# A hybrid attention block on one core: neighbourhood attention on array halves, wide probabilities scaled before they are transposed, and four more conditioning slices on TensorE

## The chip, the cores and the metric

The kernel runs on one core of one Trainium2 chip. The metric is the device time of a whole execution in microseconds (us), lower being better. The engines are TensorE (PE in the profile; PEld is its weight load), VectorE (DVE), ScalarE (ACT), GpSimd (POOL) and SyncE (SP, which only issues transfers here).

## The reference, cut to what matters

A stream of 256 latent tokens follows 256 context tokens through 4 layers of width 1024. Layers 0 and 3 mix tokens by neighbourhood attention, layer 1 by retention, layer 2 by a convolution, and each is followed by a convolutional feed-forward part. A conditioning vector gives shift, scale and gate of every part.

```python
def na_mixer(hx, hc, w_qkv, w_o, q_gain, k_gain, rpb, need_ctx):   # 16 heads of 64
    q, k, v = heads(h @ w_qkv); q, k = head_rms_norm(q), head_rms_norm(k)
    # a latent token sees its neighbourhood (with a bias from rpb) and all context tokens
    s_nb  = einsum('bhqd,bhqkd->bhqk', q_r, k_nb) * NA_SCALE + bias_r
    s_ctx = einsum('bhqd,bhkd->bhqk', q_r, kc) * NA_SCALE
    p = softmax(concatenate([s_nb, s_ctx], axis=-1))
    o = einsum(p[..., :nb], v_nb) + einsum(p[..., nb:], vc)
    yx = merge_heads(o) @ w_o
    # a context token sees all context tokens (needed in layer 0 only)
    p = softmax(einsum('bhqd,bhkd->bhqk', qc, kc) * NA_SCALE)
    yc = merge_heads(einsum(p, vc)) @ w_o
```

## The kernel before, in words

Activations lie with features on the 128 partitions and 512 tokens along the free axis: columns 0 to 255 are the context (`CT`), 256 to 511 the latent tokens (`XT`). Tokens form four blocks `b` of 128, of which 0 and 1 are context ("narrow": 256 keys) and 2 and 3 latent ("wide": 512 keys). Every projection is three fp32r products (high x high, low x high, high x low); SP brings weights in groups of 512 KB into four slots `raw`, ACT writes the high part `Whi` (line 1009) and DVE the low part `Wlo` (line 1339). Each engine's program is written out by hand, and its order is the order in which things run; semaphores tie the engines together.

**Projections of attention.** The q/k stage makes 16 tiles of 128 features (`head_sum`, line 731, sums squares of a head; DVE's `normed`, lines 1530 and 1532, normalises). It runs as four rounds of four tiles `m` with a normalisation behind each. V follows token-major (lines 581 to 583).

**Attention.** A head pair `i` (8 of them) is one row group of `QK`: head `par` = 0 in partitions 0 to 63, `par` = 1 in 64 to 127. A unit is (`par`, `b`); in layer 0 a head pair has 8 units, in layer 3 (latent tokens only) 4. For a unit POOL copies half the queries into `Qz`, whose other half is zero (line 517); PE multiplies over all 128 rows (line 762); DVE adds the bias `rel` (wide units, line 1560) and takes the negated maximum (line 1562); ACT writes the exponentials with their sum (line 1138); PE transposes them in blocks of 128 (line 770); ACT copies the result to `probT` (line 1130); PE multiplies `probT` as weights by 64 columns of `V` (line 780); DVE takes the reciprocal of the sum (line 1568) and scales into `O` (line 1570). Units run one by one, the transposes two units and the last product three units behind the scores. After the last head pair `O` is transposed (line 814), split into `Hhi` (ACT, line 1165) and `Hlo` (DVE, line 1595), and the o projection (lines 575 to 577) begins.

**Conditioning.** Its weights come in 512 KB pieces. The first slices of 128 features are made on PE at the start: line 674 uses a quarter of the columns for each piece of a product of 32x512, and line 680 transposes the result. All other pieces are "weighs" on DVE (line 1363, over 1024 columns), with a scaling on POOL (line 461) and a sum on ACT (line 1026). The constants `IN_V`, `IN_HEADS` and `IN_O` place 8 weighs in layer 0's V stage, 8 in its attention (one to a head pair) and 8 in its o projection; four weighs are one slice. The norm behind the o projection (lines 453, 455, 688 to 699) opens the feed-forward part.

## Time and profile before

| what | value |
|---|---|
| runs (three) | 2615.69 to 2620.32 us, median 2619.65 |
| time of the profiled execution / its span | 2620.63 / 2618.7 us |
| PE, PEld busy | 96%, 80% of the span |
| DVE, ACT, POOL busy | 72%, 40%, 21% |
| matrix instructions | 12948 |

The profiled execution's own time is 0.98 us above the median of the runs. Rows below give a start in us from the span's start, a duration in us, and the engine; "x4" means four instructions joined in one row, of which the duration covers all. Such durations overlap the next row on PE, since matrix products are pipelined: what a group costs is the distance from its start to the next group's start.

### The profile page before, as it was taken

Reading aid. Unit: us, or ns where it says so; the run is one execution under the profiler, and the core shown is the slowest. Engines: PE = TensorE matmul, PEld = TensorE weight load, DVE = VectorE, ACT = ScalarE, POOL = GpSimd, SP = SyncE. Lnnn points to the kernel's source line nnn. Section 1 sums busy time; section 2 is a strip of 40 time slices with the busy share of each in tenths; the row PEclk is TensorE's granted clock in tenths of the full one; section 3 lists DMA queues with packets and bytes.
Section 4 is the critical chain, followed back from the end, with each engine's and each line's share of the span. In section 5 each row is a group of like instructions: output and inputs, shape, how many; then the busy total and the mean of one; then the engine's idle time right before and its main releaser. Section 6 shows DMA issues by size and latency. Waiting matters only on the chain. (4 is left out here: it accounts for less than half of the span.)

```text
span 2618.7 us, 37653 instructions
## 1 busy us (share of the span) xinstructions
PE 2521.8 (96%) x12948; PEld 2093.5 (80%) x12948; DVE 1887.9 (72%) x2765; ACT 1044.2 (40%) x1677; POOL 557.3 (21%) x367
## 2 busy tenths in 40 slices
PE   6999989999999999999999999999999999999999
PEld 4777778888888857788888887878888887777999
DVE  4887789888974344427888768877988777756874
ACT  2336714444231123314444226543444323344543
POOL 5123243332210020022333210003333224002000
PEclk8999989999999999999999999989999999999999
DMA  8332034545632311223445531103544545311455
GB/s 265 99 123 79 32 129 143 174 167 197 210 117 96 107 62 49 88 97 137 174 168 170 188 119 57 57 17 113 169 168 169 193 155 125 105 41 65 169 184 178
DMA packets 94883, 337.39 MB, mean 129 GB/s; under 512 B 11840, under 2 KB 13632, under 8 KB 94656
## 3 DMA queue, kind: packets, MB, share of 16 engines
q1 hardware_dynamic: 64832, 231.99, 25.9%
q10 hardware_dynamic: 27072, 95.13, 10.9%
q0 software_dynamic: 2880, 8.92, 1.7%
q8 instruction: 66, 1.08, 0.2%
q14 instruction: 33, 0.27, 0.0%
HBM read 334.95 MB, written 1.05 MB: 128 GB/s over the span
## 5 line engine op out<-in xcount | busy, mean ns | idle before, releaser
L575 PE MATMUL bank<-Hhi,Whi 128*128 128x512 f32 (+1 forms) x2440 | 879.8, 361 | 46.9 <-DVE Wlo L1339 20.2
L576 PE MATMUL bank<-Hlo,Whi 128*128 128x512 f32 (+1 forms) x2440 | 863.2, 354 | 0.0
L577 PE MATMUL bank<-Hhi,Wlo 128*128 128x512 f32 (+1 forms) x2440 | 863.0, 354 | 0.0
L1339 DVE TENSOR_TENSOR Wlo<-raw,Whi 128x1024 fp32r<-128x1024 f32 x424 | 638.6, 1508 | 243.1 <-ACT Whi L1009 241.1
L1009 ACT ACTIVATE Whi<-raw 128x1024 fp32r<-128x1024 f32 x424 | 448.2, 1059 | 793.6 <-DMA raw<-in_weights 710.9
L575 PEld LDWEIGHTS bank<-Hhi,Whi 128*128 128x128 f32 x2440 | 467.4, 192 | 123.3 <-issue 41.1
L576 PEld LDWEIGHTS bank<-Hlo,Whi 128*128 128x128 f32 x2440 | 467.7, 192 | 65.9 <-issue 4.8
L577 PEld LDWEIGHTS bank<-Hhi,Wlo 128*128 128x128 f32 x2440 | 467.2, 191 | 62.2
L461 POOL TENSOR_TENSOR cond_w<-cond_w,cond 128x1024 f32<-128x1024 f32 x115 | 276.8, 2407 | 559.3 <-DVE square L1363 516.6
L575 PE MATMUL bank<-Ghi,Whi 128*128 128x512 f32 (+1 forms) x770 | 269.5, 350 | 0.0
L577 PE MATMUL bank<-Ghi,Wlo 128*128 128x512 f32 (+1 forms) x770 | 268.8, 349 | 0.0
L576 PE MATMUL bank<-Glo,Whi 128*128 128x512 f32 (+1 forms) x770 | 268.3, 348 | 0.0
L453 POOL TENSOR_TENSOR square<-X 128x512 f32<-128x512 f32 (+1 forms) x58 | 84.8, 1463 | 689.0 <-DVE X L1481 680.1
L1363 DVE SCALAR_TENSOR_TENSOR hb<-cond_w,cond 128x1024 f32<-128x1024 f32 x138 | 185.8, 1346 | 4.7
L576 PEld LDWEIGHTS bank<-Glo,Whi 128*128 128x128 f32 x770 | 144.5, 188 | 21.5
L575 PEld LDWEIGHTS bank<-Ghi,Whi 128*128 128x128 f32 x770 | 144.5, 188 | 21.4
L577 PEld LDWEIGHTS bank<-Ghi,Wlo 128*128 128x128 f32 x770 | 144.4, 188 | 21.2
L1287 ACT ACTIVATE hb<-hb 128x512 f32<-128x512 f32 (+1 forms) x88 | 51.0, 579 | 218.7 <-DVE hb L1794 218.7
L1026 ACT ACTIVATE cond_w<-cond_w 128x1024 f32<-128x1024 f32 x115 | 121.0, 1052 | 36.2 <-POOL cond_w L461 35.6
L1363 DVE SCALAR_TENSOR_TENSOR square<-cond_w,cond 128x1024 f32<-128x1024 f32 x99 | 121.2, 1224 | 11.7
L581 PE MATMUL bank<-Whi,Hhi 128*128 128x512 f32 x256 | 101.3, 396 | 2.6 <-DVE QK L1532 2.6
L1481 DVE SCALAR_TENSOR_TENSOR X<-bank,mod,X 128x256 f32<-128x256 f32 x84 | 37.4, 478 | 90.5 <-PE bank L577 90.4
(202 smaller groups left out, 3118.8 us busy)
## 6 DMA issues: line engine op xcount, KB each, us to landing
raw<-in_weights SPq DMA_DIRECT2D x424, 512.0 KB, 3.3
cond_w<-in_ada ACTq DMA_DIRECT2D x176, 512.0 KB, 3.8
ada_raw<-in_ada SPq DMA_DIRECT2D x16, 512.0 KB, 15.6
rel_in<-in_rpb POOLq DMA_DIRECT2D x48, 128.0 KB, 4.7
decay_t<-in_dist POOLq DMA_DIRECT2D x4, 640.0 KB, 4.2
X<-in_x ACTq DMA_DIRECT2D x1, 2048.0 KB, 9.6
out_y<-X SPq DMA_DIRECT2D x1, 1024.0 KB, 4.8
cos_sin<-in_rope ACTq DMA_DIRECT2D x1, 256.0 KB, 2.5
```

The lines of the kernel that those rows point to most:

```text
L453: g.tensor_tensor(square[:, c % 2, tok], X[:, c, tok], X[:, c, tok], ALU.mult).then_inc(sum_step, 1)
L461: g.tensor_tensor(w, w, cond[:, 0, :], ALU.mult).then_inc(cond_scaled, 1)
L575: t.matmul(dst, Whi[:, st.slot, w], hi, start=start, stop=False)
L576: t.matmul(dst, Whi[:, st.slot, w], lo, start=False, stop=False)
L577: return t.matmul(dst, Wlo[:, st.slot, w], hi, start=False, stop=stop)
L581: t.matmul(dst, hi, Whi[:, st.slot, w], start=start, stop=False)
L1009: a.activation(Whi[:, st.slot, :], raw[:, st.slot, :], ACT.Copy).then_inc(hi_split, 1)
L1026: a.activation(w, w, ACT.Copy, accum_out=cond_sum[:, n % COND_SLOTS, 0:1]).then_inc(cond_summed, 1)
L1287: a.activation(cv[:, k, tok], cv[:, k, tok], ACT.Gelu_apprx_tanh).then_inc(gelu_done, 1)
L1339: v.tensor_tensor(Wlo[:, st.slot, :], raw[:, st.slot, :], Whi[:, st.slot, :].bitcast(F32), ALU.subtract)\
L1363: last = v.scalar_tensor_tensor(spare[:, :, :].rearrange("p k t -> p (k t)"), w, 1.0, cond[:, r, :], ALU.mult, ALU.mult, accum_out=cond_su ...
L1481: last = v.scalar_tensor_tensor(X[:, m, hs], src[:, hs], gate, X[:, m, hs], ALU.mult, ALU.add)
```

## The change

Attention is planned by a class `Heads`: units in the order head pair, block, head, so that the two heads of one block stand next to each other. A step works on such a pair of units.

- Scores are taken straight from `QK`, head 0 from partitions 0 to 63 and head 1 from 64 to 127, each over half of the array's rows; `Qz` and its copies go.
- For wide units one DVE operation adds the bias, negates, and takes the minimum (`tensor_tensor_reduce`, over 512 keys, the bias of the context keys being zeros); ACT's exponential has scale -1 there. Narrow units keep their reduction.
- The reciprocal is taken of the two sums of a step at once, and the probabilities are scaled before the transposes: wide ones by DVE in place, narrow ones by POOL.
- ACT copies the transposed wide units, DVE the narrow ones. The last product has 64 columns of `V` as weights and 256 queries as moving columns, head 0 into the upper half of a bank's partitions and head 1 into the lower: its result already has features on partitions. `O` and its transposes go; `out_high` and `out_low` split each result while attention runs.
- Transposes stand three steps behind the scores, and the last product of a head pair's stream follows every second step.
- Four more slices of conditioning (`ADA_QK`) go to PE, one in each of the four rounds of layer 0's q/k stage: `ada_slice` (8 products of 32 columns by 512, four of them side by side on column quarters) behind tile 1, its transposes ahead of the last `head_sum`; SP loads 2 MB for each. DVE copies the rows and stores them (`ada_rows`, `ada_store`). PE waits for the last store ahead of V. The 8 weighs in attention and the 8 in the o projection go (`IN_HEADS`, `IN_O`), and ACT loads the first conditioning pieces only behind `ada_used` of the fourth slice.
- In layer 0 ACT evicts V's blocks 2 and 3 (`evict_v`), which DVE did. The convolution's filter is loaded at the start of retention.

```diff
-ADA_FIRST = 4
+ADA_START = 4
+ADA_QK = 4
+ADA_FIRST = ADA_START + ADA_QK
 QUAD = P // 4
 COND_SLOTS = 3
 PER_LAP = 3
 IN_V = 8
-IN_HEADS = 8
-IN_O = (0, 0, 1, 1, 2, 2, 3, 4)
+IN_HEADS = 0
+IN_O = ()
...
+    def __init__(self, layer):
+        self.last = layer == DEPTH - 1
+        self.blocks = (2, 3) if self.last else (0, 1, 2, 3)
+        self.units = [(i, par, b) for i in range(C) for b in self.blocks for par in range(2)]
+        self.n = len(self.units)
+        self.u0 = 8 * C if self.last else 0
+        self.wide0 = 4 * C if self.last else 0
+        per = 2 * len(self.blocks)
+        self.ends = {n: (n // per, 0 if n % 8 == 3 and not self.last else 1) for n in range(3, self.n, 4)}
...
-                        pool.wait_ge(scored, SCORED0 + u0 - n_units + n_units // 2 * (par + 1) + n_units * i)
-                        half = slice(64 * par, 64 * par + 64)
-                        g.tensor_copy(Qz[half, par, tok], QK[half, i, tok]).then_inc(q_staged, 1)
...
+                h = Heads(layer)
+                for n, (i, par, b) in enumerate(h.units):
+                    if b < 2:
+                        pool.wait_ge(inverted, h.u0 // 2 + n // 2 + 1)
+                        g.tensor_scalar(prob[n % 6][:, CT], prob[n % 6][:, CT], rinv[:, n // 2 % 4, par:par + 1], None,
+                                        ALU.mult).then_inc(narrow_scaled, 1)
...
+            def ada_slice(n):
+
+                for k in range(C):
+                    if k % 2 == 0:
+                        pe.wait_ge(ada_loaded[k // 2], 16 * (n + 1))
+                    last = ada_product(bank[6], k, ada_ring[:, k // 2, 512 * (k % 2):512 * (k % 2) + 512])
+                last.then_inc(ada_used, 1)
...
+                            if layer == 0 and n < ADA_QK and m == 1:
+                                ada_slice(n)
+                            if layer == 0 and n < ADA_QK and m == 3:
+                                ada_cols(ADA_START + n)
                         head_sum(3, 8 * nth + 3 + 4 * i, tok)
+                if layer == 0:
+                    pe.wait_ge(mod_ready, 4 * ADA_FIRST)
                 tokens_major(p["v"], 2, p["mix_tile"] + 16)
 
 
...
-                    pe.wait_ge(exped, u0 + u + 1 + n_units * i)
-                    t.matmul(bank[u % 4][:, keys], Qz[:, par, P * b:P * b + P], QK[:, 8 + i, keys],
+                    half = slice(64 * par, 64 * par + 64)
...
+                    if n >= 4:
+                        pe.wait_ge(exped, h.u0 + n - 3)
+                    t.matmul(bank[n % 4][:, keys], QK[half, i, P * b:P * b + P], QK[half, 8 + i, keys],
                              start=True, stop=True).then_inc(scored, 1)
...
+                def turn(n):
+                    i, par, b = h.units[n]
+                    if b < 2:
+                        pe.wait_ge(narrow_scaled, h.narrow(n))
+                    else:
+                        pe.wait_ge(wide_scaled, h.wide(n))
+                    if n >= 2:
+                        copies(n - 2)
+                    for kb in range(2 if b < 2 else TB):
...
+                    turned = wide_pT[:, h.parity(i), :, :, :] if stream else narrow_pT
+                    n_keys = TB if stream else 2
                     for kb in range(n_keys):
-                        last = t.matmul(bank[6 + u % 2][:, 0:NA_HD], probT[:, u % 2, P * kb:P * kb + P],
-                                        V[:, kb, bass.ts(2 * i + par, NA_HD)], start=kb == 0, stop=kb == n_keys - 1)
+                        for par in range(2):
+                            last = t.matmul(bank[h.out_bank(i, stream)][64 * par:64 * par + 64, 0:CTX],
+                                            V[:, kb, NA_HD * (2 * i + par):NA_HD * (2 * i + par + 1)],
+                                            turned[:, par, kb, :], start=kb == 0, stop=kb == n_keys - 1)
...
+                for s in range(h.n // 2 + 4):
+                    if s == 0:
+                        pe.wait_ge(tile_free, FREE0 + p["mix_tile"] + 2 * C + TB)
+                    if s == 1:
+                        pe.wait_ge(tile_free, FREE0 + p["mix_tile"] + 2 * C + 2 * TB)
+                    for n in (2 * s, 2 * s + 1):
+                        if n < h.n:
+                            scores(n)
+                    for n in (2 * s - 6, 2 * s - 5):
+                        if 0 <= n < h.n:
+                            turn(n)
+                    if 2 * s - 7 in h.ends:
+                        attend(2 * s - 7)
...
+                def evict_v(y):
+                    act.wait_ge(weights_used, p["v"] + 4 * y + 4)
+                    for b in (2, 3):
+                        a.activation(V[:, b, 512 * y:512 * (y + 1)], bank[V_BANKS[y][b]][:, :], ACT.Copy)\
+                            .then_inc(v_made, 1)
...
+                    act.wait_ge(ada_used, ADA_QK)
+                    for n in range(COND_SLOTS):
+                        load_weights(n)
...
+                def exponentials(n):
+                    i, par, b = h.units[n]
...
+                    act.wait_ge(peaked, h.u0 + n + 1)
+                    if n >= 6:
+                        act.wait_ge(p_turned, h.u0 + n - 5)
+                    a.activation(prob[n % 6][:, keys], bank[n % 4][:, keys], ACT.Exp, bias=peak[:, n % 4:n % 4 + 1],
+                                 scale=1.0 if b < 2 else -1.0, accum_out=psum_p[:, n // 2 % 4, par:par + 1]).then_inc(exped, 1)
+
+                def out_high(n):
+                    i, stream = h.ends[n]
+                    act.wait_ge(attended, h.u0 // 4 + n // 4 + 1)
+                    a.activation(Hhi[:, i, XT if stream else CT], bank[h.out_bank(i, stream)][:, 0:CTX], ACT.Copy)\
+                        .then_inc(h_hi, 1)
+
+                for s in range(h.n // 2 + 5):
+                    for n in (2 * s, 2 * s + 1):
+                        if n < h.n:
+                            exponentials(n)
+                    if 2 * s - 9 in h.ends:
+                        out_high(2 * s - 9)
+                    for n in (2 * s - 6, 2 * s - 5):
+                        if 0 <= n < h.n and h.units[n][2] >= 2:
+                            copy_turned(n)
...
+                            if layer == 0 and n < ADA_QK and m == 2:
+                                ada_rows(n)
                             if m:
                                 normed(m - 1, k - 1, i, tok)
+                        if layer == 0 and n < ADA_QK:
+                            ada_store(ADA_START + n)
...
-                        sx = bank[u % 4][:, XT].rearrange("p (r k) -> p r k", k=GRID_W)
-                        v.tensor_tensor(sx, sx, rel[:, 2 * i + par, a0:a0 + 4, :], ALU.add).then_inc(biased, 1)
-                        dve.wait_ge(biased, b0 + 2 * par + b - 1 + x_units * i)
-                    v.tensor_reduce(peak[:, u % 4:u % 4 + 1], bank[u % 4][:, keys], axis=AX, op=ALU.max,
-                                    negate=True).then_inc(peaked, 1)
...
-                    v.tensor_scalar(O[:, i, b, NA_HD * par:NA_HD * (par + 1)], bank[6 + u % 2][:, 0:NA_HD],
-                                    rinv[:, u % 4:u % 4 + 1], None, ALU.mult).then_inc(o_stored, 1)
...
+                        sx = bank[n % 4][:, :].rearrange("p (s k) -> p s k", s=2)
+                        v.tensor_tensor_reduce(sx, sx, bias, -1.0, 3e38, ALU.add, ALU.min,
+                                               accum_out=peak[:, n % 4:n % 4 + 1]).then_inc(peaked, 1)
+                    else:
+                        v.tensor_reduce(peak[:, n % 4:n % 4 + 1], bank[n % 4][:, keys], axis=AX, op=ALU.max,
+                                        negate=True).then_inc(peaked, 1)
...
+                def invert_sums(s):
+                    dve.wait_ge(exped, h.u0 + 2 * s + 2)
+                    if s >= 4 and h.units[2 * s - 8][2] < 2:
+                        dve.wait_ge(narrow_scaled, h.narrow(2 * s - 7))
+                    v.reciprocal(rinv[:, s % 4, :], psum_p[:, s % 4, :]).then_inc(inverted, 1)
+                    if h.units[2 * s][2] >= 2:
+                        dve.wait_ge(inverted, h.u0 // 2 + s + 1)
+                        for par in range(2):
+                            p = prob[(2 * s + par) % 6]
+                            v.tensor_scalar(p, p, rinv[:, s % 4, par:par + 1], None, ALU.mult).then_inc(wide_scaled, 1)
...
+                    v.tensor_copy(narrow_pT[:, par, :, P * b:P * b + P],
+                                  bank[4 + n % 2][:, CT].rearrange("p (k q) -> p k q", q=P)).then_inc(narrow_copied, 1)
...
+                for s in range(h.n // 2 + 5):
+                    if 2 * s < h.n:
+                        peaks(2 * s)
+                    if 2 * s < h.n:
+                        peaks(2 * s + 1)
+                    if 0 < s <= h.n // 2:
+                        invert_sums(s - 1)
+                    for n in (2 * s - 6, 2 * s - 5):
+                        if 0 <= n < h.n and h.units[n][2] < 2:
+                            copy_turned(n)
+                    if 2 * s - 9 in h.ends:
+                        out_low(2 * s - 9)
```

On PE, at the end of the q/k stage, where V begins (before; `na_sq` holds squares, `Whi` the V weights from here on as moving operand):

```order
L575 MATMUL bank<-Hhi,Whi 128x512
L576 MATMUL bank<-Hlo,Whi 128x512
L577 MATMUL bank<-Hhi,Wlo 128x512
L731 MATMUL bank<-na_sq,one_head 128x512 x2
L151 REGISTER_ALU
L151 COMPARE_AND_BRANCH
L581 MATMUL bank<-Whi,Hhi 128x512
L582 MATMUL bank<-Whi,Hlo 128x512
```

The same place after the change:

```order
L616 MATMUL bank<-Hhi,Whi 128x512
L617 MATMUL bank<-Hlo,Whi 128x512
L618 MATMUL bank<-Hhi,Wlo 128x512
L780 MATMUL bank<-na_sq,one_head 128x512
L729 MATMUL bank<-ident,hb 128x128 x4
L780 MATMUL bank<-na_sq,one_head 128x512
L622 MATMUL bank<-Whi,Hhi 128x512
L623 MATMUL bank<-Whi,Hlo 128x512
```

The two products with `na_sq` now have four transposes of conditioning rows (`hb`) between them, and the first product of V stands behind a wait for DVE's last store.

On PE within layer 0's attention, before (one unit's scores, an earlier unit's transposes, a still earlier unit's last product, in turns):

```order
L770 MATMUL bank<-ident,prob 128x128 x4
L780 MATMUL bank<-V,probT 128x64 x2
L762 MATMUL bank<-QK,Qz 128x256
L770 MATMUL bank<-ident,prob 128x128 x4
L780 MATMUL bank<-V,probT 128x64 x4
L762 MATMUL bank<-QK,Qz 128x512
L770 MATMUL bank<-ident,prob 128x128 x2
L780 MATMUL bank<-V,probT 128x64 x4
L762 MATMUL bank<-QK,Qz 128x512
```

After the change (`square`, `root`, `total` and `hb` are here names under which the six probability buffers appear):

```order
L814 MATMUL bank<-QK 128x512 x2
L833 MATMUL bank<-ident,square 128x128 x8
L814 MATMUL bank<-QK 128x512 x2
L833 MATMUL bank<-ident,root 128x128 x2
L833 MATMUL bank<-ident,total 128x128 x2
L847 MATMUL bank<-wide_pT,V 64x256 x8
L814 MATMUL bank<-QK 128x256 x2
L833 MATMUL bank<-ident,hb 128x128 x4
L814 MATMUL bank<-QK 128x256 x2
L833 MATMUL bank<-ident,square 128x128 x8
```

Two scores now follow each other, then the transposes of two units, and only every second step has products of the last kind, with 256 columns in place of 64.

On DVE within layer 0's attention, before:

```order
L1570 TENSOR_SCALAR O<-bank,rinv 128x64
L1560 TENSOR_TENSOR bank<-bank,rel 128x256
L1562 TENSOR_REDUCE peak<-bank 128x1
L1568 RECIPROCAL rinv<-psum_p 128x1
L1570 TENSOR_SCALAR O<-bank,rinv 128x64
L1560 TENSOR_TENSOR bank<-bank,rel 128x256
L1562 TENSOR_REDUCE peak<-bank 128x1
L1568 RECIPROCAL rinv<-psum_p 128x1
```

After the change ("ISA" is the fused operation, and the row behind it reads its result back):

```order
L1634 RECIPROCAL rinv<-psum_p 128x2
L1653 TENSOR_TENSOR Hlo<-bank,Hhi 128x256
L1624 ISA bank,peak<-bank,rel 128x512
L1624 ISA peak 128x1
L1624 ISA bank,peak<-bank,rel 128x512
L1624 ISA peak 128x1
L1634 RECIPROCAL rinv<-psum_p 128x2
L1639 TENSOR_SCALAR hb<-hb,rinv 128x512 x2
L1646 COPY narrow_pT<-bank 128x2x128 x2
```

The addition and the reduction of a wide unit are one operation; the scaling moved from 64 columns of the result to 512 of the probabilities; copies of narrow units and the low part of the result are new here.

## Rows read from the trace of the kernel before

**Rows 1.** The page's busy times: engine, us, share of the span, instructions.
```profile
PE 2521.8 (96%) x12948; PEld 2093.5 (80%) x12948; DVE 1887.9 (72%) x2765; ACT 1044.2 (40%) x1677; POOL 557.3 (21%) x367
```

**Rows 2.** Windows: us, PE, PEld, DVE, ACT, POOL, PEclk, DMA share, GB/s.
```profile
142.00:174.00 32.00, 32.00 (x135) 24.92 (x134) 27.29 (x19) 9.07 (x12) 3.72 (x3) 1.00 0.25 87
207.00:212.00 5.00, 3.98 (x9) 2.48 (x9) 2.48 (x7) 3.56 (x7) 2.31 (x4) 0.50 0.35 129
208.00:316.00 108.00, 107.36 (x698) 85.92 (x699) 81.93 (x245) 79.53 (x212) 28.37 (x24) 0.98 0.13 44
```

**Rows 3.** Timeline of PE in layer 0's attention.
```profile
240.37 0.65 PE L762 MATMUL bank<-QK,Qz 128*128 x2
240.86 0.60 PE L770 MATMUL bank<-ident,prob 128*128 128x128 f32 x4
241.30 0.56 PE L780 MATMUL bank<-V,probT 128*128 x4
241.69 0.65 PE L762 MATMUL bank<-QK,Qz 128*128 x2
...
242.62 1.00 PE L780 MATMUL bank<-V,probT 128*128 x8
243.46 1.08 PE L762 MATMUL bank<-QK,Qz 128*128 x2
244.37 0.38 PE L770 MATMUL bank<-ident,prob 128*128 128x128 f32 x2
...
253.53 0.65 PE L762 MATMUL bank<-QK,Qz 128*128 x2
```

**Rows 4.** Groups of DVE in attention: shapes, count | busy us, mean ns | idle before.
```profile
L1562 DVE TENSOR_REDUCE peak<-bank 128x1 f32<-128x512 f32 x32 | 22.1, 691 | 1.1
...
L1560 DVE TENSOR_TENSOR bank<-bank,rel 128x256 f32<-128x256 f32 x32 | 13.8, 432 | 11.9 <-PE bank L762 11.0
L1562 DVE TENSOR_REDUCE peak<-bank 128x1 f32<-128x256 f32 x32 | 13.4, 418 | 2.1 <-PE bank L762 2.0
...
L1363 DVE SCALAR_TENSOR_TENSOR hb<-cond_w,cond 128x1024 f32<-128x1024 f32 x8 | 9.8, 1225 | 0.3
```

**Rows 5.** Timeline of PE at the first conditioning slices.
```profile
26.13 2.00 PE L674 MATMUL bank<-ada_raw,csilu 128*32 128x512 f32 x16
28.06 0.66 PE L680 MATMUL bank<-ident,rows 128*128 128x128 f32 x4
```

**Rows 6.** Groups of DVE in the convolution layer.
```profile
L1706 DVE TENSOR_SCALAR Wc<-U,cvf 128x512 f32<-128x512 f32 x8 | 3.9, 485 | 1.1 <-DVEq L1700 0.3
```

**Rows 7.** Timeline of DVE, then of POOL, behind the o projection.
```profile
361.00 2.18 DVE L1363 SCALAR_TENSOR_TENSOR hb<-cond_w,cond 128x1024 f32<-128x1024 f32 x1
...
359.76 2.34 POOL L455 TENSOR_TENSOR total<-total,square 128x512 f32<-128x512 f32 x1
```

**Rows 8.** Timeline of PE, then of DVE, where V begins.
```profile
157.98 1.55 PE L731 MATMUL bank<-na_sq,one_head 128*128 128x512 f32 x3
...
163.96 0.75 DVE L1532 SCALAR_TENSOR_TENSOR QK<-bank,qk_gain,na_root 128x512 f32 x1 [0.15 <-DVE na_root L1530]
```

**Rows 9.** Timelines: first exponential and first o product, layer 0, then layer 3.
```profile
210.13 0.47 ACT L1138 ACTIVATE prob<-bank,peak 128x256 f32<-128x256 f32 x1
...
323.68 0.50 PE L575 MATMUL bank<-Hhi,Whi 128*128 128x512 f32 x1 [1.73 <-DVE Hlo L1595]
...
2319.16 0.69 ACT L1138 ACTIVATE prob<-bank,peak 128x512 f32<-128x512 f32 x1 [3.45 <-DVE peak L1562]
...
2391.95 0.39 PE L575 MATMUL bank<-Hhi,Whi 128*128 128x256 f32 x1 [0.93 <-DVE Hlo L1595]
```

**Rows 10.** Timelines of PE: end of the o projection's norm, layer 0; the same stage, layer 2.
```profile
393.21 0.70 PE L699 MATMUL bank<-root,one 128*128 128x256 f32 x2 [0.24 <-DVE root L1398]
...
1756.80 0.77 PE L575 MATMUL bank<-Hhi,Whi 128*128 128x512 f32 x1 [3.10 <-DVE Hlo L1739]
...
1813.96 0.70 PE L699 MATMUL bank<-root,one 128*128 128x256 f32 x2 [0.24 <-DVE root L1398]
```

287 lines of the change are left out of this document (117 added, 170 removed).

## The prediction

> **What bounds the kernel now.** I read the page first. PE is busy for 96% of the span, DVE for 72%, ACT for 40% and POOL for 21% [rows 1]: a change pays where it takes work from PE, or where it ends a wait of PE. The windows say whether that holds stage by stage. In the q/k stage PE is busy for 32.00 of 32.00 us with DVE at 27.29, so anything put on PE there is paid in full; in layer 0's attention PE is busy for 107.36 of 108.00 us, with DVE at 81.93 and ACT at 79.53 [rows 2]. So attention before is a PE stage too.
>
> The timeline then prices each kind of work in it, by the distance from one group's start to the next's [rows 3]: wide scores 0.91 us (243.46 to 244.37), narrow scores 0.49 (240.37 to 240.86), four transposes 0.44 (240.86 to 241.30), hence two of them 0.22, the last product of a narrow unit 0.39 (241.30 to 241.69), of a wide one 0.84 (242.62 to 243.46). A head pair is 4 x (0.91 + 0.44 + 0.84) + 4 x (0.49 + 0.22 + 0.39) = 13.16 us, and the trace has 253.53 - 240.37 = 13.16. From the first exponential to the first o product it is 323.68 - 210.13 = 113.55 us in layer 0 and 2391.95 - 2319.16 = 72.79 in layer 3 [rows 9].
>
> **The change part by part.**
>
> *Four slices on PE in the q/k stage.* A slice has 8 products of 32 columns, four of them side by side. Before, 16 matmul records (8 products of two passes each) take 28.06 - 26.13 = 1.93 us up to the transposes [rows 5]; that is two rounds of four at the 0.91 of a product over 512 columns [rows 3], and about 0.1 left for going over to another kind. I add 0.44 for the transposes and 0.45 for four changes of kind into and out of the tiles. 4 x 2.8 = +11.2 us; without the changes it would be +9.5, with 0.25 each +13.5. No wait hides it, since PE has none there [rows 2]. SP's 8 MB more come on DMA queues at a share of 0.25. DVE's copies and stores, some 1.5 us a slice, fit beside its 27.29 of 32.
>
> *The wait ahead of V.* PE now stands until the fourth slice is stored, and this store is behind the third normalisation on DVE. PE's last squares end at about 159.5 (157.98 + 1.55), the normalisation at 164.7 (163.96 + 0.75) [rows 8]; with the wait for its input and a store of 0.6, PE starts at 165.3: 5.8 us idle. Behind a similar hole the granted clock is 0.50 in 207 to 212, the 1.2 GHz level of the two [rows 2], so I add 2 us: +7.8. The bounds are +5.8 and +10. Behind PE's wait stands all of V, and nothing else can go ahead of it.
> The Trainium skill ("TensorE: Matmul & The Clock Gate", Part 1) says too that an idle TensorE falls to its lower clock and has to be busy before it is given back; the trace agrees by that 0.50.
>
> *Attention of layer 0.* Per head pair PE does: scores of two heads on row halves. If they run side by side, two wide for the time of one: 2 x 0.91 + 2 x 0.49 = 2.80. Transposes stay: 4 x 0.44 + 4 x 0.22 = 2.64. The last products move 256 columns in two halves of the array's columns: four pairs for the latent stream and two for the context, each at the 0.49 of a product over 256 columns [rows 3]: 2.94. Ten changes between row halves, whole array and column halves at 0.15 add 1.5. Sum 9.9 us, 2.5 a step. No row shows row halves; column quarters side by side are in [rows 5], which is why I take the overlap, with both bounds kept.
> The Trainium skill ("TensorEngine Tiling (Array Packing)", "Key Properties") says that a change of tiling mode drains the engine. By the trace it costs 0.1 us at most at the one place where it happens [rows 5]; at nothing the step would be 2.1 us on PE, and VectorE would set it.
>
> DVE per head pair: four fused operations. Bounds are one pass of the reduction, 0.69, and the two operations it replaces, 0.43 + 0.69 = 1.12 [rows 4]. I take the lower, since it is one pass over 512 columns, and 0.08 for reading its result: 3.08. Four narrow reductions at 0.42 [rows 4] 1.68, four reciprocals at 0.15 0.6, four wide scalings at 0.485 from SBUF [rows 6] 1.94, four narrow copies and two low parts, each 256 columns and put at that 0.42, 2.52. Sum 9.8 us, 2.45 a step. ACT keeps its exponentials and loses half of its copies, so it stays below its 79.53 of 108. POOL has two narrow scalings in every second step, and they are wanted two steps later.
> PE and DVE are then equal, and each waits for the other through four banks of scores. I put the step at 2.7 us. With 32 steps, and 7.5 us for the last step's exponentials, scaling, transposes, copies, product and splitting: 31 x 2.7 + 7.5 = 91.2 against 113.55, -22.3 us. The transposes of `O`, and the 1.73 us ahead of the first o product [rows 9], go with it, since the split is made under way.
>
> *The o projection of layer 0* loses 8 weighs. The same stage with no weighs, in layer 2, takes 1813.96 - 1756.80 = 57.2 us from its first product to its norm's last; in layer 0 it takes 393.21 - 323.68 = 69.5 [rows 10, 9]. -12.3 us. It can't be more, as the rest is PE's own products; it could be some 3 less if other waits there stay.
>
> *Attention of layer 3.* Only wide units, 16 steps of two. PE per head pair: 1.82 + 1.76 + 1.96 + 5 x 0.15 = 6.3; DVE 4 x (0.77 + 0.485) + 0.3 + 0.42 = 5.7. Step 3.15 and 2.87; I take 3.3. 15 x 3.3 + 7.5 = 57 against 72.79: -15.8 us.
>
> *What costs nothing.* V's blocks are evicted by ACT, which is a quarter busy there; the convolution's filter arrives more than 1000 us before its use; the first conditioning pieces are fetched at about 158, and DVE has its first use near 170. Were that cover gone, the first weigh would be late by the transfer, a few us on DVE, not on PE.
>
> Sum: 11.2 + 7.8 - 22.3 - 12.3 - 15.8 = -31.4. From the profiled execution's 2620.6 that is 2589, or 2588 against the median of the runs, which is 1 us lower.
>
> **The rivals.**
>
> *Even faster (0.14).* DVE's minimum sets the step in layer 0 (2.45) and PE's in layer 3 (3.1), with changes of mode nearly free: -30.1 and -18.8, sum -42, 2578.
>
> *VectorE becomes the bound (0.09).* For it: it is 2.45 of a 2.5 us step. Either the fused operation takes its upper bound, 1.12 plus 0.08, which gives steps of 2.9 and 3.75; or its operations from SBUF stand while POOL works, as a weigh took 2.18 us beside POOL's addition [rows 7] against a mean of 1.23 [rows 4]. Together I put steps at 3.1 and 4.1: -10 and -3.8, sum -7, 2613. Against it: in layer 3 POOL has no unit to scale.
> The Trainium skill ("SBUF — State Buffer", "SBUF: two separate sides") calls this an exclusive lock on a shared pair of ports; the 2.18 us agree with it.
>
> *Row halves do not run side by side, column halves do (0.11).* Scores cost 5.6 in place of 2.8: steps of 3.2 and 4.1. -6.9 and -3.8, sum -4, 2616. For it: the trace has columns side by side only.
> The Trainium skill ("TensorE: Matmul & The Clock Gate", Part 3) gives row tiles a gain near their number, which speaks against this rival; no row here shows it.
>
> *Slower: neither halves overlap (0.05).* Each product holds the array for its whole time. PE has 5.6 + 2.64 + 5.88 + 1.5 = 15.6 us per head pair, 3.9 a step, and 5.0 in layer 3: +14.9 and +10.0, with +6.7 from the rest makes +32, 2652. It decides from about 24% above my steps, 3.34 us in layer 0 with 4.08 in layer 3, where the whole change is worth nothing. Against it: four column quarters ran at four times the speed [rows 5].
>
> *Slower: attention at the 1.2 GHz level (0.03).* The present stage has 0.98 granted [rows 2]; the new one has small waits in each step. Matmul time doubled gives steps of 4.6 and 5.9: +36 and +23, sum +66, 2686.
>
> **How the numbers follow.** The forecast has 0.58. 0.2% of this time, 5.2 us, is about what a measurement can tell from no change. Faster: the forecast, the faster rival, and the two cases near 2613 and 2616 as far as they fall below 2614.4: 0.58 + 0.14 + 0.07 + 0.03 = 0.82. Within: the rest of those two, 0.10. Slower: the two last, 0.08. The range goes from 2572, a little below the faster rival for the bounds of the first two terms, to 2616, which takes in the case of VectorE and most of that of the row halves, and leaves out both slow ones.
>
> **What would show it.** In the profile after: in the q/k stage four gaps between tile products of about 2.8 us each; a wait of PE for a store on DVE of 5 to 6 us ahead of V, with a lower granted clock behind it; scores of two heads 0.9 us from start to start of the next group, not 1.8; the fused operation at 0.7 us and not 1.1; steps of 2.7 and 3.3 us from one pair's scores to the next pair's; o projection of 57 us. I am wrong first if steps are above 3, and then the rows of PE's waits must say whether DVE or PE's own products hold it.

## The result and the profile after

The changed kernel takes 2592.38 us (median of four runs, 2588.88 to 2594.36), against 2619.99 for the kernel before on the same occasions: a ratio of 0.9891, with an interval of 0.9872 to 0.9910. It is faster, by more than the 0.2% of the prediction, and inside the stated range. The profiled execution took 2591.67 us with a span of 2589.9, 28.8 below the span before.

The first part of the page of the changed kernel, which answers to [rows 1]:

```profile
PE 2467.2 (95%) x12660; PEld 2020.6 (78%) x12660; DVE 1827.2 (71%) x2671; ACT 1020.1 (39%) x1641; POOL 544.8 (21%) x355
```

PE lost 54.6 us of busy time, about twice what the kernel gained; the rest came back as waits. PE's waits between 60 and 240 us of the changed kernel (engine and line that waited and what for: us in total, times, longest):

```profile
PE bank L814 <- DVE V L1575: 6.9, 1, 6.9
PE bank L729 <- DVE hb L1438: 5.6, 1, 5.6
PE bank L622 <- DVE mod L1446: 5.2, 1, 5.2
PE bank L814 <- ACT hb L1201: 3.4, 1, 3.4
```

The second was not in my sum; the third is the predicted wait ahead of V. The first stands between V and the first scores, the last behind these; before there was one wait of 4.95 us.

The timeline of PE in one head pair of layer 0, which answers to [rows 3] (`square`, `root`, `total` and `hb` are probability buffers here):

```profile
300.67 0.70 PE L814 MATMUL bank<-QK 64*128 64x256 f32 x4
301.30 0.66 PE L833 MATMUL bank<-ident,hb 128*128 128x128 f32 x4
301.88 0.70 PE L814 MATMUL bank<-QK 64*128 64x256 f32 x4
303.62 1.06 PE L833 MATMUL bank<-ident,square 128*128 128x128 f32 x8 [1.04 <-DVE narrow_pT L1646]
304.62 1.08 PE L847 MATMUL bank<-narrow_pT,V 128*64 128x256 f32 x8
305.63 1.13 PE L814 MATMUL bank<-QK 64*128 64x512 f32 x4
306.69 0.65 PE L833 MATMUL bank<-ident,root 128*128 128x128 f32 x4
307.18 0.60 PE L833 MATMUL bank<-ident,total 128*128 128x128 f32 x4
307.71 1.13 PE L814 MATMUL bank<-QK 64*128 64x512 f32 x4
309.94 0.90 PE L833 MATMUL bank<-ident,hb 128*128 128x128 f32 x4 [1.10 <-ACT wide_pT L1191]
310.77 1.95 PE L847 MATMUL bank<-wide_pT,V 128*64 128x256 f32 x16
312.65 0.70 PE L814 MATMUL bank<-QK 64*128 64x256 f32 x4
```

Two wide scores take 1.06 us (305.63 to 306.69), where one took 0.91 before. A head pair is 312.65 - 300.67 = 11.98 us, of which 1.04 + 1.10 = 2.14 are waits, each ahead of transposes and each for a copy out of the bank that they need. PE's own work is 9.84 us, and I had summed 9.9.

The window of that attention (columns as in [rows 2]) shows no engine full:

```profile
234.15:324.00 89.85, 72.71 (x456) 39.55 (x458) 60.65 (x195) 56.62 (x169) 29.16 (x32) 0.97 0.02 5
```

Where the 28.8 us went, stage by stage in the two traces:

| stretch | forecast | measured |
|---|---|---|
| q/k stage of layer 0, up to PE's hole | +11.2 | +12.7 (171.66 for 158.96) |
| hole ahead of V | +5.8 | +5.15 |
| V's own products | +2 | +1.7 (45.8 for 44.1) |
| V's end to the first exponential | 0 | +4.5 (11.6 for 7.05) |
| attention, layer 0 | -22.3 | -14.8 (98.75 for 113.55) |
| o projection, layer 0 | -12.3 | -15.7 (53.84 for 69.5) |
| attention, layer 3 | -15.8 | -13.9 (58.89 for 72.79) |
| everything else | 0 | -8.4 |
| sum | -31.4 | -28.75 |

The last row but one has no part of the change in it. It sits almost wholly in the down projections of the feed-forward parts: 5.9 us in layers 0 to 2 and 1.5 us in layer 3. Two products of that stage in the kernel before, 36 products apart:

```profile
663.80 0.39 PE L577 MATMUL bank<-Ghi,Wlo 128*128 128x512 f32 x1
...
672.20 0.39 PE L577 MATMUL bank<-Ghi,Wlo 128*128 128x512 f32 x1
```

and in the changed kernel:

```profile
664.25 0.39 PE L618 MATMUL bank<-Ghi,Wlo 128*128 128x512 f32 x1
...
672.49 0.39 PE L618 MATMUL bank<-Ghi,Wlo 128*128 128x512 f32 x1
```

8.40 us became 8.24, 0.2333 and 0.2289 us a product, in code that the change does not touch and at the same granted clock (1.00 from 660 to 680 us in both traces). Each down projection of layers 0 to 2 takes 115.31 us for 117.26, in all 5.9 us. Layer 3's took 60.54 for 62.07, but other kernels of the next section whose buffers lie like the changed kernel's take 62.07 again (a_both_first, a_all), so this 1.5 us belongs to the one execution and not to the change.

### The profile page after: what moved, and what is told of

Same layout as the page of the kernel before. It is cut to its first block and busy times, and to the rows that moved or that the text cites. A ratio compares the mean times of both kernels' runs of the same rounds, so it can differ in the third digit from the quotient of the medians.

```text
span 2589.9 us, 36031 instructions
## 1 busy us (share of the span) xinstructions
PE 2467.2 (95%) x12660; PEld 2020.6 (78%) x12660; DVE 1827.2 (71%) x2671; ACT 1020.1 (39%) x1641; POOL 544.8 (21%) x355
## 5 line engine op out<-in xcount | busy, mean ns | idle before, releaser
L616 PE MATMUL bank<-Hhi,Whi 128*128 128x512 f32 (+1 forms) x2440 | 876.8, 359 | 38.6 <-DVE Hlo L1480 15.8
L512 POOL TENSOR_TENSOR cond_w<-cond_w,cond 128x1024 f32<-128x1024 f32 x107 | 258.2, 2413 | 643.3 <-DVE square L1417 514.8
L1417 DVE SCALAR_TENSOR_TENSOR hb<-cond_w,cond 128x1024 f32<-128x1024 f32 x114 | 150.3, 1319 | 3.8
L1076 ACT ACTIVATE cond_w<-cond_w 128x1024 f32<-128x1024 f32 x107 | 112.5, 1051 | 36.3 <-POOL cond_w L512 35.4
## 6 DMA issues: line engine op xcount, KB each, us to landing
ada_raw<-in_ada SPq DMA_DIRECT2D x16, 512.0 KB, 15.7
```

What stands on the lines that cost most here:

```text
L512: g.tensor_tensor(w, w, cond[:, 0, :], ALU.mult).then_inc(cond_scaled, 1)
L616: t.matmul(dst, Whi[:, st.slot, w], hi, start=start, stop=False)
L1076: a.activation(w, w, ACT.Copy, accum_out=cond_sum[:, n % COND_SLOTS, 0:1]).then_inc(cond_summed, 1)
L1417: last = v.scalar_tensor_tensor(spare[:, :, :].rearrange("p k t -> p (k t)"), w, 1.0, cond[:, r, :], ALU.mult, ALU.mult, accum_out=cond_su ...
```

## The experiments

Ratios are to the kernel before; the changed kernel's is 0.9891. Between kernels of one group the difference is taken through these ratios and, below 0.3%, from the traces.

**1. The address of the large buffers.** In the programs as built every buffer starts at a multiple of 32 bytes in its partition. The change makes small tensors 32 bytes a partition larger in all, which moves every buffer behind them: `Ghi`, which the down projections move through the array, starts at byte 117664 before the change (a multiple of 64, plus 32) and at 117696 after it (a multiple of 64). Four kernels put an unused tensor ahead of it, two in the kernel before and two in the changed one.

```diff
         sd4 = sb("sd4", [P, TB])
+        sb("pad", [P, 8])
```

(`[P, 4]`, 16 bytes, in a_align64 and b_shift16. Since buffers start at multiples of 32 bytes, these 16 bytes move `Ghi` by 32 as well.)

> The kernel before with one unused tensor of 32 bytes a partition, so that the large buffers of the feed-forward part begin 32 bytes later, where the changed kernel has them. Theory (the 1.9 us that each feed-forward part of layers 0 to 2 gained come from the address of its moving operand): the 36 products from 671.50 on take 8.24 us and not 8.40, and the whole is 6 to 8 us below the kernel before, with attention as it was. Rival (the gain comes from the changed kernel's other traffic or timing): 8.40 as before, and no difference.

Measured: 0.9964 (0.9946 to 0.9982), some 9 us faster with nothing but 32 unused bytes; the span fell from 2618.7 to 2610.4. The same two products in its trace are 8.24 us apart:

```profile
664.20 0.39 PE L578 MATMUL bank<-Ghi,Wlo 128*128 128x512 f32 x1
...
672.44 0.39 PE L578 MATMUL bank<-Ghi,Wlo 128*128 128x512 f32 x1
```

> The changed kernel with the same 32 bytes more, which puts the large buffers where they have the remainder by 64 bytes of the kernel before. Theory of the address: the down projections go back to 0.2333 us a product, and the whole is 6 to 8 us above the changed kernel. Rival (only the absolute place or something else counts): no difference.

Measured: 0.9928 (0.9911 to 0.9945), 10 us above the changed kernel, and 8.40 us for the 36 products.

> The changed kernel with 16 bytes more, which puts the large buffers at a multiple of 64 bytes. Theory of the address: the pitch of the down projections falls from 0.2289 us to the 0.2275 that products from Hhi have, some 2 us less in all; if any remainder but that of before is equally good: no difference.

Measured: 0.9922 (0.9905 to 0.9939), and the slow pitch again, 8.40 us. The edit did not do what was expected of it: it took `Ghi` from a multiple of 64 bytes to 117728, the place that it has in a_shift32. The question of a further gain at a multiple of 64 was answered already, since the changed kernel stands at one.

> The kernel before with 16 unused bytes a partition, which gives the large buffers the one remainder by 64 bytes not seen yet, 32; the others were 16 (0.2333 us a product in the down projection), 48 (0.2289) and 0 (0.2333). If the upper half of 64 bytes is the good one: 0.2289, and 6 to 10 us below the kernel before. If only 48 is: 0.2333, and no difference.

Measured: 0.9967 (0.9956 to 0.9978), 8.24 us. The remainders 16, 48, 0 and 32 in this expectation are wrong, and it tries no new place: its buffers lie exactly as in b_shift32, as those of a_align64 lie as in a_shift32. What was tested is two remainders, with a repeat:

| `Ghi` starts at | by 64 bytes | kernels | 36 products | a down projection |
|---|---|---|---|---|
| 117664 | 32 | before | 8.40 us | 117.26 us |
| 117728 | 32 | a_shift32, a_align64 | 8.40 us | 117.53 us |
| 117696 | 0 | changed, b_shift32, b_shift16 | 8.24 us | 115.31 us |

The address theory holds, in a simpler form: a multiple of 64 bytes is the fast place, 32 bytes beside it the slow one, and shifts to either side of it agree. No remainder but these two was tried. Whether it is the address of the moving operand that counts, or that of another buffer which moved with it (`Glo`, `QK` and `V` did), was not separated. So 5.9 of the 28 us are an accident of the layout as far as the products show it. The whole kernels differ by more, 8 to 10 us by the four ratios, but the narrowest of their intervals reaches from 6 to 12 us, and the traces don't place the rest.

**2. The copies that PE waits for in attention.** The changed kernel's ACT in the same head pair (start, duration):

```profile
304.63 0.48 ACT L1201 ACTIVATE square<-bank,peak 128x256 f32<-128x256 f32 x1 [1.47 <-DVE peak L1627]
...
305.09 0.46 ACT L1201 ACTIVATE square<-bank,peak 128x256 f32<-128x256 f32 x1
...
305.54 1.08 ACT L1191 ACTIVATE wide_pT<-bank 128x512 f32<-128x512 f32 x2
```

The wide units of 303.62 were turned by 304.6, but their copies start at 305.54, behind two exponentials that wait for DVE. ACT's program has the exponentials of a step first. The experiment swaps that, and on DVE puts the narrow copies ahead of reciprocal and scaling:

```diff
+                    for n in (2 * s - 6, 2 * s - 5):
+                        if 0 <= n < h.n and h.units[n][2] >= 2:
+                            copy_turned(n)
                     for n in (2 * s, 2 * s + 1):
                         if n < h.n:
                             exponentials(n)
                     if 2 * s - 9 in h.ends:
                         out_high(2 * s - 9)
-                    for n in (2 * s - 6, 2 * s - 5):
-                        if 0 <= n < h.n and h.units[n][2] >= 2:
-                            copy_turned(n)
```

> The changed kernel with two orders swapped in attention: ACT copies transposed wide units ahead of the step's exponentials, DVE copies narrow ones ahead of the reciprocal and the wide scaling. Theory (PE's two waits of 1.04 to 1.10 us in a head pair are for copies queued behind other work on ACT and DVE): both waits go and no new one comes, a head pair falls from 11.97 us to about 10, layer 3's from 7.23 to about 6.3; 16 + 7 = some 20 us less in all. Rival (the copies are now early but the exponentials late, and scores wait for them two steps on): the waits move to the scores, and a head pair stays at 11.5 or more.

Measured: 0.9846 (0.9829 to 0.9862). Attention of layer 0 takes 91.45 us for 98.75, layer 3's from first scores to first o product 54.8 for 62.7: 15.2 us, with 20 expected. The whole kernel gained less, 12 us by the ratios and by the spans, since in this trace V starts 4.3 us later: the wait at the first slice is 8.4 us, for 5.6 in the changed kernel (experiment 4). PE in a head pair:

```profile
293.79 1.13 PE L814 MATMUL bank<-QK 64*128 64x512 f32 x4
...
300.43 0.74 PE L833 MATMUL bank<-ident,hb 128*128 128x128 f32 x4 [0.33 <-DVE narrow_pT L1646]
...
302.75 1.06 PE L833 MATMUL bank<-ident,square 128*128 128x128 f32 x8 [0.94 <-DVE narrow_pT L1646]
...
304.75 1.13 PE L814 MATMUL bank<-QK 64*128 64x512 f32 x4
```

The wait for ACT is gone and PE takes 304.75 - 293.79 = 10.96 us for a head pair; two waits for DVE's narrow copies, 1.27 us, stay. The theory holds for ACT, whose copies cost PE's transposes 7.7 us of waits in layer 0's attention and now nothing. It fails for DVE: PE's waits for narrow copies went from 9.2 us in 9 waits to 10.6 us in 16, since the copies still stand behind the peaks, which wait for fresh scores. The two swaps came in one edit, so what DVE's does by itself is not shown. The rival is out, as a head pair is below 11.5 us. With this order the attention of layer 0 takes what was forecast (91.2).

**3. The store ahead of V.**

```diff
+                            if layer == 0 and n == ADA_QK - 1 and m == 3:
+                                ada_store(ADA_START + n)
                             if m:
                                 normed(m - 1, k - 1, i, tok)
-                        if layer == 0 and n < ADA_QK:
+                        if layer == 0 and n < ADA_QK - 1:
                             ada_store(ADA_START + n)
```

> The changed kernel with DVE's store of the fourth slice ahead of the normalisation that it stood behind. Theory (PE's 5.15 us ahead of V are that reciprocal of 3.35 and its product of 0.75 on DVE, nothing else): the wait falls to about 1 us, V starts 4 us earlier, and with a shorter hole the slow stretch at a granted clock of 0.50 behind it shrinks; 4 to 6 us less. Rival (V also waits for banks that the normalisations free): the wait stays near 5 under another name.

Measured: 0.9869 (0.9848 to 0.9889). The wait fell from 5.15 to 1.1 us, and V's own products from 45.8 to 43.8 us, with PE at a granted clock of 1.00 behind the short hole. The theory holds for the wait. The 6 us in the ratios can't be put down to it alone, since this trace has a smaller wait in the q/k stage too (0.6 for 5.6 us), for which the next experiment stands.

Windows of the changed kernel around the hole (columns as in [rows 2]):

```profile
171.00:176.00 5.00, 0.66 (x2) 0.00 (x0) 4.85 (x3) 2.40 (x4) 0.00 (x0) 0.82 0.88 283
176.00:181.00 5.00, 4.19 (x10) 3.33 (x11) 4.86 (x6) 0.00 (x0) 0.00 (x0) 0.50 0.36 139
181.00:186.00 5.00, 5.00 (x24) 4.12 (x23) 2.08 (x3) 0.00 (x0) 2.39 (x1) 1.00 0.09 21
```

A window of a_store_early behind its hole:

```profile
171.00:174.00 3.00, 3.00 (x15) 2.46 (x14) 2.96 (x3) 0.00 (x0) 0.00 (x0) 1.00 0.54 179
```

Behind a hole of 5.15 us V begins at the 1.2 GHz level (0.50) for about 4 us; behind one of 1.1 us it stays at 2.4 GHz.

**4. The wait at the first slice.** DVE of the changed kernel, then its POOL:

```profile
79.19 4.74 DVE L1393 TENSOR_TENSOR Wlo<-raw,Whi 128x1024 fp32r<-128x1024 f32 x1
83.86 0.68 DVE L1438 COPY hb<-bank 128x512 f32<-128x512 f32 x1
...
76.12 6.72 POOL L546 TENSOR_TENSOR rel<-rel_in,mask 128x3072 f32<-128x3072 f32 x1 [8.54 <-DMA rel_in<-in_rpb]
```

The split of two SBUF operands, 1.23 us elsewhere, ends 1.1 us after POOL's addition (83.93 and 82.84), as if it did all its work behind it. In the trace of a_both_first it took 6.60 us and ended 1.1 us after POOL again (82.17 and 81.08). The Trainium skill ("SBUF — State Buffer", "SBUF: two separate sides") says that GpSimd and such a VectorE operation exclude each other for a whole instruction, and these rows agree. The copy of the slice's rows stands behind the split, and PE behind the copy.

```diff
+                            if layer == 0 and n < ADA_QK and m == 2:
+                                ada_rows(n)
                             split(Step(p["mix"] + 8 * nth + m, 4, i))
-                            if layer == 0 and n < ADA_QK and m == 2:
-                                ada_rows(n)
```

> The changed kernel with DVE's copy of a slice's rows ahead of the weight split of the same tile. Theory (PE's 5.64 us at the transposes of the first slice are for that copy, which stands behind a split stretched from 1.23 to 4.74 us by POOL's addition of the bias tables): the wait falls below 1 us; V starts up to 5 us earlier. Rival (the stretched split makes PE wait elsewhere, since its tile needs the low part too): the wait moves to the next product with that split, and V starts as before.

Measured: 0.9880 (0.9850 to 0.9910), V starts at 176.63 (176.81 before the edit). PE's waits between 60 and 185 us:

```profile
PE bank L622 <- DVE mod L1446: 5.2, 1, 5.2
PE bank L616 <- DVE Hlo L1480: 4.8, 1, 4.8
PE bank L616 <- DVE Wlo L1393: 2.2, 1, 2.2
```

The wait for the copy is gone, and one for the split itself took its place, as the rival said: PE needs the low part too. But it is 2.2 us and not 5.6. The other wait, of 4.8 us, is no successor of it: it stands ahead of everything that the edit touches. The changed kernel has such a wait for `Hlo` too, 1.7 us, which the window from 60 us on leaves out as it ends at 59.53. PE's rows in the trace of the experiment:

```profile
59.53 0.58 PE L616 MATMUL bank<-Hhi,Whi 128*128 128x256 f32 x1 [4.84 <-DVE Hlo L1480]
...
74.84 1.92 PE L715 MATMUL bank<-ada_ring,csilu 128*32 128x512 f32 x16
```

PE reaches the first slice at 74.84 us here and at 69.63 in the changed kernel, and yet V starts at the same time. From the first slice's products to the second's it takes 24.8 us for 30.2. That is the gain of the theory, but it may come from the late arrival as well, since POOL's addition runs from 72.1 to 78.8 us in this trace. So the experiment does not decide between theory and rival. What it shows is how the collision varies: PE's wait at the first slice was between 0.4 and 8.4 us in the traces of these kernels, with a split beside POOL's addition stretched in every one of them, the kernel before included (3.79 us there).

**5. Do row halves run side by side?**

```diff
+                    half = slice(0, 64)
                     t.matmul(bank[n % 4][:, keys], QK[half, i, P * b:P * b + P], QK[half, 8 + i, keys],
```

> The changed kernel with the scores of both heads taken from partitions 0 to 63, so that the second head's scores are wrong: the same products, but never on different halves of the array's rows. Theory (two heads' scores run side by side on row halves): four records over 512 columns take 1.8 us in place of 1.06, those over 256 columns 1.0 in place of 0.6, a head pair of layer 0 grows by 2 x 0.75 + 2 x 0.4 = 2.3 less what the waits of 2.1 us absorb, layer 3's by 1.5; at least 15 us more in all. Rival (records of 64 rows are simply shorter, no overlap): the four records stay at 1.06 and the time does not change.

Measured: 0.9958 (0.9942 to 0.9973), 17 us above the changed kernel. In its timeline:

```profile
302.71 1.98 PE L815 MATMUL bank<-QK 64*128 64x512 f32 x4
304.62 1.09 PE L834 MATMUL bank<-ident,square 128*128 128x128 f32 x8
...
315.50 1.98 PE L815 MATMUL bank<-QK 64*128 64x512 f32 x4
```

1.91 us for the four records against 1.06: they run side by side on different halves and one after the other on one half, a gain of 1.8 for two halves. The rival of the prediction is excluded. A head pair is 12.79 us, only 0.8 longer than with halves, since waits of 2.1 us shrank to 0.3; the rest of the 12 us in layer 0 goes with its first 26 us of attention, which had a granted clock of 0.66.

**6. The fused bias and maximum.**

```diff
-                        v.tensor_tensor_reduce(sx, sx, bias, -1.0, 3e38, ALU.add, ALU.min,
-                                               accum_out=peak[:, n % 4:n % 4 + 1]).then_inc(peaked, 1)
+                        v.tensor_tensor(sx, sx, rel[:, 2 * i + par, a0:a0 + 4, :], ALU.add).then_inc(biased, 1)
+                        dve.wait_ge(biased, j + 1 + h.wide(n))
+                        v.tensor_reduce(peak[:, n % 4:n % 4 + 1], bank[n % 4][:, keys], axis=AX, op=ALU.max,
+                                        negate=True).then_inc(peaked, 1)
```

> The changed kernel with the fused bias and maximum split into the two operations of before (0.43 and 0.69 us, against 0.70 with 0.08 to read the result back). Theory (the peaks are in the chain peaks, exponentials, copies, that makes PE wait in attention, on both engines): a head pair of layer 0 grows from 11.97 by 4 x 0.35 = 1.4 us, layer 3's from 7.23 by up to the same; 15 to 22 us more. Rival (DVE has slack, being busy 61 of 90 us in layer 0's attention): less than 5 us more.

Measured: 1.0005 (0.9992 to 1.0018). All that the change gained is gone, 30 us for 15 to 22 expected. Attention of layer 0 takes 115.05 us, layer 3's 76.2 for 62.7. PE's timeline in layer 3, one wait and what follows it:

```profile
2354.66 1.12 PE L833 MATMUL bank<-ident,hb 128*128 128x128 f32 x8 [1.89 <-ACT wide_pT L1191]
2355.71 3.41 PE L847 MATMUL bank<-wide_pT,V 128*64 128x256 f32 x16
2359.05 1.30 PE L814 MATMUL bank<-QK 64*128 64x512 f32 x4
```

Three windows of the same kernel in layer 0 (a head pair; a group of 16 products at the low level; one at the high level):

```profile
305.79:320.20 14.41, 11.40 (x67) 5.98 (x65) 9.77 (x26) 7.53 (x23) 3.65 (x5) 0.88 0.01 2
311.92:315.23 3.31, 3.31 (x17) 1.71 (x17) 2.51 (x7) 1.45 (x4) 0.00 (x0) 0.55 0.03 5
326.13:328.01 1.88, 1.88 (x18) 1.06 (x17) 1.81 (x6) 1.50 (x4) 0.00 (x0) 1.00 0.00 0
```

The longer peaks lengthen PE's waits from 1.10 to 1.89 us, which is the chain that was expected, though with 0.8 us a head pair of layer 3 in place of up to 1.4. What was not: behind some of these waits the granted clock falls to the 1.2 GHz level, and the same 16 records take 3.4 us in place of 1.9. The mean granted clock in layer 3's attention is 0.83, against 1.00 in the changed kernel. The two attention stages are 29.5 us longer, and only 7 us of that are waits for the copies (32.1 for 25.1 us): PE's busy time went from 79.1 to 90.5 us in layer 0 and from 48.3 to 58.9 in layer 3, with the same products. So three quarters of the loss go with the clock. The rival of attention at the 1.2 GHz level, to which I gave 0.03, came true in part with 0.8 us more of wait a head pair.

**7. Half of the trade undone.**

```diff
-ADA_QK = 4
+ADA_QK = 2
-IN_O = ()
+IN_O = (0, 0, 1, 1, 2, 2, 3, 4)
```

> Half of the trade undone: two slices on TensorE in the q/k stage instead of four, and the 8 weighs back in the o projection. Theory (a weigh in the o projection costs PE more than its share of a slice): the q/k stage gets 2 x 2.4 = 4.8 us shorter, the o projection 12 to 16 us longer; in all 8 to 11 us more than the changed kernel. Rival (the o projection is shorter for another reason, the split of the attention's result being done early): it stays at 54 us, and the kernel gets 5 us faster than the changed one.

Measured: 0.9913 (0.9891 to 0.9935), some 6 us above the changed kernel, 7.0 by the spans. The o projection with its norm is back at 69.05 us (53.84), and PE waits there between 215 and 400 us again for:

```profile
PE bank L737 <- POOL total L506: 6.0, 1, 6.0
PE bank L616 <- DVE Wlo L1393: 3.6, 2, 1.9
```

So the weighs cost 15.2 us there, with waits for POOL and the weight split; the rival is out. V starts 8.5 us earlier, 5.15 of them because the last two rounds carry no slice and the hole is gone; PE reached the first slice 5 us later in this trace, so the rest does not measure the two slices. The theory holds for each stage, but the whole is 6 to 7 us and not the 8 to 11 expected: I had left the hole out of that sum.

**8. The start of attention.**

```diff
                     evict_v(1)
-                    sum_products(IN_V - 1)
-                    reload(IN_V - 1, p["cond_end"])
...
+                    if layer == 0 and s == 1:
+                        sum_products(IN_V - 1)
+                        reload(IN_V - 1, p["cond_end"])
```

> The changed kernel with ACT's last conditioning sum, and the load behind it, moved behind the exponentials of the second step of layer 0's attention. Theory (the first exponential, 11 us behind V's last product against 7 before, waits for this sum, which waits for POOL, and for a table load of 1.28 us behind it): it starts 3 us earlier, and the whole is 3 us less. Rival (DVE's late copies of V set the start): less than 1 us.

Measured: 0.9880 (0.9859 to 0.9900). From V's start to the first exponential it takes 53.8 us for 57.3, and to the first o product 152.6 for 156.1: 3.5 us, as expected; a total of 3 us is too small for the ratios to tell.

**9. All together.**

> The changed kernel with the swapped orders of copies in attention, the early store of the fourth slice, the early row copies and the late last sum together. Theory (four separate waits on PE's chain, so that their prices add): 15 for the copies, 4 to 6 for the store, 3.5 for the sum, and up to 5 for the rows, in all 22 to 29 us below the changed kernel, a ratio of 0.978 to 0.981 to the kernel before. Rival (some share one cover): less than 18 us.

Measured: 2565.12 us, 0.9793 (0.9771 to 0.9815), as expected, some 26 us below the changed kernel by the ratios; 56 us, 2.1%, below the kernel before. The first exponential comes at 219.20, the first o product at 310.65, the end of the span at 2558.2. The rival is out. That the early row copies have a part in it is not shown: the wait at the first slice is 0.4 us here, but it was 0.6 in a_store_early without them. This is the fastest version of the study. What is left in its attention are DVE's narrow copies (10.3 us in layer 0) and 7.0 us of PE ahead of the first scores.

## Why the prediction was right, point by point

**The total** came out at 2592 for 2588, but not term by term. The stages that the forecast named gave 20.4 us and not 31.4; the missing 11 us were made up by luck for 8.4, of which 5.9 are the place of the buffers and 1.5 one fast execution of layer 3's down projection. Without that the time would be near 2601, still in the range. The mechanisms in the sum were right; the terms that were mis-sized, and one that was left out, are named below.

**The q/k stage** (+11.2, measured +12.7) was right in size with other parts. A slice costs 1.85 us for its products (155.53 to 157.38), 0.43 for its transposes and some 0.15 for going over and back, 2.4 and not 2.8; a whole round shows the same, 27.85 us for 25.41. The four changes of kind at 0.45 in all were mis-sized, some three times too dear.

```profile
155.53 1.92 PE L715 MATMUL bank<-ada_ring,csilu 128*32 128x512 f32 x16
157.38 0.50 PE L616 MATMUL bank<-Hhi,Whi 128*128 128x512 f32 x1
```

The first slice's wait of 5.64 us was missed by the step that said DVE's copies fit beside its other work; the kernel before had 3.3 us of waits in the stage.

**The hole ahead of V** was right (5.15 for 5.8, and 1.7 for 2 by the clock).

**The start of attention**, which I left out of the sum as unchanged, cost 4.5 us: the step that failed is the line that V's eviction on ACT is free. DVE waited there for ACT (`v_made`):

```profile
211.89 1.22 DVE L1393 TENSOR_TENSOR Wlo<-raw,Whi 128x1024 fp32r<-128x1024 f32 x1 [7.28 <-ACT V L1150]
```

It came late with its last weigh and its own copies, POOL and ACT with the sum behind it, and the first exponential stood behind that sum; experiment 8 took 3.5 us of it back. That the eviction began this chain is read from the rows; no run moved it back to DVE.

**Attention of layer 0** was right in each engine's sum: PE 9.84 for 9.9; row halves side by side; fused operation 0.64 and 0.14 for reading back, for the assumed 0.69 and 0.08; scaling 0.485, copies 0.42. What failed is the term for coupling: 2.7 a step, where it was 3.0, which is 9.1 us in 31 steps; the 7.5 us for the last step were 1.6 too many. I had set 0.2 us a step between the sums without asking what is queued ahead of the copies. On ACT it is exponentials, and experiment 2 takes 7.3 of the missing 7.5 us back with the order of the copies: PE's waits for ACT are 7.7 us less and those for DVE 1.4 us more.

**Layer 3** came within 1.9 us by two errors that nearly cancel. The step was 3.6 us for 3.3, which is 4.7 us in 15 steps and has the same cause; the 7.5 us for its start and end were 2.8 too many. With the copies put first a head pair takes 2329.59 - 2323.55 = 6.04 us, without a wait, and the stage 50.85 us where I forecast 57, so PE's own 6.3 a head pair was too dear as well:

```profile
2323.55 1.13 PE L814 MATMUL bank<-QK 64*128 64x512 f32 x4
...
2329.59 1.13 PE L814 MATMUL bank<-QK 64*128 64x512 f32 x4
```

**The o projection** gave 3.4 us more than forecast. The stage of layer 2 that I took as its price starts behind a wait of 3.10 us with a first product of 0.77 us [rows 10], the 1.2 GHz level; its first 14 products are 0.43 us apart and the later ones 0.23, which is 2.8 of the 3.4 us. The one in layer 0 starts with 0.50, and its granted clock is 1.00.

**The rivals.** Row halves without overlap: excluded by experiment 5. VectorE as the bound: its operations had the durations of the forecast, and DVE is busy for 60.65 of the 89.85 us of layer 0's attention; but by experiment 6 a dearer peak reaches PE's chain in part (0.8 us a head pair of layer 3), although DVE is not full. The clock at 1.2 GHz: it did not come in the changed kernel (0.98 and 1.00 in the two attention stages), but experiment 6 shows it near.

## What to carry to other kernels

When the engines' sums in a pipelined step are nearly equal, the step is set by the order inside each engine's program: put what frees a bank for the next transposes ahead of what produces work for two steps later. Before trusting a difference of a few tenths of a per cent, compare the pitch of stages that the change does not touch, and move all buffers by 32 bytes: here that was worth at least a fifth of the whole gain. Look up where the buffers really start before drawing on their addresses, for a tensor of 16 bytes moved them by 32. Small waits can cost more by the granted clock than by themselves (22 of 29.5 us in experiment 6), so an operation's price is to be judged with the waits that it makes.

## What the runs showed of the hardware

- fp32r products over 512 columns whose large buffers start at a multiple of 64 bytes have a pitch of 0.2289 us, and 32 bytes beside it one of 0.2333 us, in the down projections of six kernels (three of each).
- Scores of two heads on the two row halves of the array take 1.06 us for four records over 512 columns, on one half 1.91 us (experiment 5).
- One wait of 1.89 us in each head pair of layer 3's attention goes with a granted clock of 0.83 on average; one of 1.10 us leaves it at 1.00. The same 16 records take 1.9 and 3.4 us.
- A DVE operation on two SBUF operands that meets POOL's addition over 3072 columns ends 1.1 us behind it, however early it was issued (4.74 and 6.60 us for 1.23).
